# RWKV gate product in split operands with its last 32 rows stacked three times, and rate products without 64 unread columns

## The reference, cut to what matters

```python
xx = time_shift(x) - x
xr, xw, xk, xv, xa, xg = [x + xx * mu[n] for n in range(6)]
r, k, v = jnp.einsum('nbtc,ncd->nbtd', jnp.stack([xr, xk, xv]), w_rkv)
w = -jax.nn.softplus(-(w0 + jnp.tanh(xw @ w1) @ w2)) - 0.5
a = jax.nn.sigmoid(a0 + (xa @ a1) @ a2)
g = jax.nn.sigmoid(xg @ g1) @ g2          # g1: 1024 x 160, g2: 160 x 1024
...
_, y = lax.scan(step, S0, ...)            # per head, state 64 x 64
y = group_norm(y) * gn_g + gn_b + bonus
return (y * g) @ w_o
```

## Time and profile before

| | |
|---|---|
| median of 3 runs | 1249.38 us (1249.12 to 1252.03) |
| the profiled execution | 1249.55 us, span 1247.4 us |
| mean granted TensorE clock | 0.981 |
| TensorE busy | 1179.5 us, 95% of the span |
| VectorE busy | 749.7 us, 60% |
| ScalarE busy | 596.4 us, 48% |
| GpSimd busy | 107.1 us, 9% |

### The profile page before, as it was taken

One profiled execution on the slowest core, in us unless ns is written; L12 is line 12 of the kernel. 1 busy time (PEld: TensorE's weight loads), 2 busy tenths in 40 slices (PEclk: granted clock), 3 DMA queues, 4 the chain that ended last, 5 costly groups with the idle time before them and its releaser, 6 DMA issues.

```text
span 1247.4 us, 24447 instructions
## 1 busy us (share of the span) xinstructions
PE 1179.5 (95%) x10438; PEld 1054.7 (85%) x10438; DVE 749.7 (60%) x1078; ACT 596.4 (48%) x837; POOL 107.1 (9%) x87
## 2 busy tenths in 40 slices
PE   4999989989999999999999999799999998999997
PEld 4897777669999989877899999599988787999996
DVE  7888665364554466775555545767587553655554
ACT  4574543354434355554644344475555554544343
POOL 0032253501100000220010000000000000000000
PEclk9999999989999999999899999899999999999999
DMA  8431011046454545232455446335433342455550
GB/s 324 170 115 70 4 50 51 16 175 233 177 195 181 214 145 203 102 136 102 169 202 184 187 177 228 135 136 203 143 116 123 115 180 85 172 200 191 181 200 34
DMA packets 29417, 187.86 MB, mean 151 GB/s; under 512 B 3344, under 2 KB 5264, under 8 KB 8080
## 3 DMA queue, kind: packets, MB, share of 16 engines
q1 hardware_dynamic: 26544, 176.94, 38.6%
q10 hardware_dynamic: 2784, 9.60, 2.2%
HBM read 185.49 MB, written 1.05 MB: 150 GB/s over the span
## 4 chain that ended last, share of the span: by engine, by line
PE 83%; DVE 9%; ACT 5%; issue 2%; DMA 0%; POOL 0%; DVEq 0%; ACTq 0%; SPq 0%; POOLq 0%
PE ps L1914 24%; PE ps L1916 23%; PE ps L1915 23%; DVE w_lo L1248 2%; ACT w_hi L575 1%; PE ps L2032 1%; PE ps L2216 1%; ACT ma_s L986 1%; PE ps L2221 1%; PE ps L2218 1%; DVE mix_lo L1683 1%; DVE x_tm L1482 1%; PE ps L2362 1%; PE ps L2164 1%; PE ps L2612 1%
## 5 line engine op out<-in xcount | busy, mean ns | idle before, releaser
L1248 DVE TENSOR_TENSOR w_lo<-w_raw,w_hi 128x2048 fp32r<-128x2048 f32 x160 | 373.5, 2350 | 179.1 <-ACT w_hi L575 178.5
L1914 PE MATMUL ps<-x_hi,w_hi 128*128 128x256 f32 x1344 | 382.9, 285 | 4.2 <-DVE x_lo L1520 2.2
L575 ACT CAST w_hi<-w_raw 128x2048 fp32r<-128x2048 f32 x158 | 300.7, 1906 | 177.8 <-PE ps L1916 174.4
L1915 PE MATMUL ps<-x_lo,w_hi 128*128 128x256 f32 x1344 | 379.3, 282 | 0.0
L1916 PE MATMUL ps<-x_hi,w_lo 128*128 128x256 f32 x1344 | 379.2, 282 | 0.0
L1914 PEld LDWEIGHTS ps<-x_hi,w_hi 128*128 128x128 f32 x1344 | 257.2, 191 | 11.3 <-issue 9.5
L1915 PEld LDWEIGHTS ps<-x_lo,w_hi 128*128 128x128 f32 x1344 | 257.1, 191 | 2.2 <-issue 0.7
L1916 PEld LDWEIGHTS ps<-x_hi,w_lo 128*128 128x128 f32 x1344 | 257.0, 191 | 0.0
L1914 PE MATMUL ps<-w_hi,hid_hi 128*128 128x512 f32 x304 | 119.8, 394 | 0.1
L1916 PE MATMUL ps<-w_hi,hid_lo 128*128 128x512 f32 x304 | 119.4, 393 | 0.0
L1915 PE MATMUL ps<-w_lo,hid_hi 128*128 128x512 f32 x304 | 118.4, 390 | 0.0
(11 more groups left out here) (367 smaller groups left out, 1716.8 us busy)
## 6 DMA issues: line engine op xcount, KB each, us to landing
w_raw<-in_weights SPq DMA_DIRECT2D x164, 1024.0 KB, 4.8
xt<-in_xT SPq DMA_DIRECT2D x2, 512.0 KB, 5.7
x_tm<-in_x SPq DMA_DIRECT2D x1, 1024.0 KB, 4.8
gain<-in_mix_g ACTq DMA_DIRECT2D x2, 512.0 KB, 4.6
gain<-in_mix_b ACTq DMA_DIRECT2D x2, 512.0 KB, 5.6
gain<-in_ffn_g ACTq DMA_DIRECT2D x2, 512.0 KB, 7.1
gain<-in_ffn_b ACTq DMA_DIRECT2D x2, 512.0 KB, 8.8
gain<-in_mem ACTq DMA_DIRECT2D x1, 1024.0 KB, 4.8
```

Of the source, the lines that this page charges most:

```text
L575: nc.scalar.copy(w_hi[:, i % WS, :], w_raw[:, i % RAW, :]).then_inc(hi_done, 1)
L1248: V.tensor_tensor(w_lo[:, i % WS, :], w_raw[:, i % RAW, :], w_hi[:, i % WS, :].bitcast(F32), ALU.subtract).then_inc(lo_done, 1)
L1914: nc.tensor.matmul(out, hi_l, hi_r, start=start, stop=False)
L1915: nc.tensor.matmul(out, hi_l, lo_r, start=False, stop=False)
```

## The change

The gate product is computed in split operands. The 128 rows take three fp32r products with `g2_hi`, `g2_lo`, `sig_hi` and `sig_lo`. The 32 rows take one product: hi, lo and hi of the activations stand under each other in 96 rows of `sig_b`, and hi, hi and lo of the weights in 96 rows of `g2b_s`, so that one contraction over 96 rows adds all three terms. For that `load_g` brings the 32 rows three times. ScalarE (`gate_high`) rounds and VectorE (`gate_low`) subtracts, in slot 5 of the next group's loop, and after the loop for group 3; the activations are split once, in slot 5 of g = 0. The raw `g2`, `g2b`, `sig_g`, `sig_g2` and `y_last` now lie in tiles that are free by then (`sw`, `sa_m`, `av`), so the first gate load waits for `S_BK` of group 0, and each later one for the subtraction of the group before.

In `S_BA0` and `S_BA1` the moving operand leaves out its first 64 columns, which nobody reads: 192 columns in place of 256. `S_KA0` and `S_KA1` keep 256.

```diff
+LORA_B = GLORA - P
+GB = 3 * LORA_B
...
-            sig_g = sb("sig_g", [P, T], where=a_rw)
-            sig_g2 = sb("sig_g2", [GLORA - P, T], where=a_rw)
+            sig_hi = sb("sig_hi", [P, T], F32R, a_rw)
+            sig_b = sb("sig_b", [GB, T], F32R, a_rw)
...
-                for dst, src in ((g2, d["g2"][0:P]), (g2b, d["g2"][P:GLORA])):
-                    sp.dma_start(dst[:, :], src[:, at]).then_inc(gate_lora_loaded, 16)
+                sp.dma_start(g2, d["g2"][0:P, at]).then_inc(gate_lora_loaded, 16)
+                for n in range(3):
+                    sp.dma_start(g2b[LORA_B * n:LORA_B * n + LORA_B], d["g2"][P:GLORA, at]).then_inc(gate_lora_loaded, 16)
...
-                if i == 11:
-                    sp.wait_ge(lora1_mm, 2)
-                    sp.wait_ge(mix_lo_done, 4)
-                    load_g(0)
+            sp.wait_ge(side_ready, side_at(0, S_BK) + 1)
+            load_g(0)
...
-                sp.wait_ge(side_ready, side_at(g - 1, S_G) + 1)
+                sp.wait_ge(gate_lo_done, g)
                 load_g(g)
...
+                    if (g, k) == (0, C_SA0):
+                        act.wait_ge(sig_lo_done, 1)
...
+            def gate_high(g):
+                if g:
+                    act.wait_ge(side_ready, side_at(g - 1, S_G) + 1)
+                act.wait_ge(gate_lora_loaded, 64 * (g + 1))
+                nc.scalar.copy(g2_hi[:, :], g2)
+                nc.scalar.copy(g2b_s[:, :], g2b[0:GB]).then_inc(gate_hi_done, 1)
...
+                    if g and slot == 5:
+                        gate_high(g - 1)
+                    elif slot == 5:
+                        nc.scalar.copy(sig_hi[:, :], sig_g)
+                        nc.scalar.copy(sig_b[2 * LORA_B:GB, :], sig_g2)
+                        nc.scalar.copy(sig_b[0:LORA_B, :], sig_g2).then_inc(sig_hi_done, 1)
...
             side_step(3, S_BK)
+            gate_high(3)
...
+            def gate_low(g):
+                dve.wait_ge(gate_hi_done, g + 1)
+                V.tensor_tensor(g2_lo[:, :], g2, g2_hi[:, :].bitcast(F32), ALU.subtract)
+                low = g2b_s[2 * LORA_B:GB, :]
+                V.tensor_tensor(low, g2b[2 * LORA_B:GB], low.bitcast(F32), ALU.subtract).then_inc(gate_lo_done, 1)
...
+                    if g and slot == 5:
+                        gate_low(g - 1)
+                    elif slot == 5:
+                        dve.wait_ge(sig_hi_done, 1)
+                        V.tensor_tensor(sig_lo[:, :], sig_g, sig_hi[:, :].bitcast(F32), ALU.subtract)
+                        V.tensor_tensor(sig_b[LORA_B:2 * LORA_B, :], sig_g2, sig_b[0:LORA_B, :].bitcast(F32), ALU.subtract)\
+                         .then_inc(sig_lo_done, 1)
...
+            gate_low(3)
...
-                    pe.wait_ge(gate_lora_loaded, 32 * (g + 1))
+                    pe.wait_ge(sig_lo_done, 1)
+                    pe.wait_ge(gate_lo_done, g + 1)
                     for t in range(TT):
-                        mm(z[:, T * t:T * t + T], sig_g[:, tok(t)], g2[:, :], start=True, stop=False)
-                        last = mm(z[:, T * t:T * t + T], sig_g2[:, tok(t)], g2b[:, :], start=False, stop=True)
+                        three(z[:, T * t:T * t + T], sig_hi[:, tok(t)], sig_lo[:, tok(t)], g2_hi[:, :], g2_lo[:, :], True, False)
+                        last = mm(z[:, T * t:T * t + T], sig_b[:, tok(t)], g2b_s[:, :], start=False, stop=True)
...
+                    c0 = HB if k in (S_BA0, S_BA1) else 0
...
-                            last = mm(both[q][:, T * m:T * m + T], src[f, 2 * m + t, :],
-                                      ar[f, 2 * g + m, t, :, :].rearrange("p s c -> p (s c)"), start=True, stop=True)
+                            last = mm(both[q][:, T * m + c0:T * m + T], src[f, 2 * m + t, :],
+                                      ar[f, 2 * g + m, t, :, :].rearrange("p s c -> p (s c)")[:, c0:T], start=True, stop=True)
```

More of the change, by code:

```diff
@@ L229, in build @@
                 akrk_b = sb("akrk_b", [P, TT, 4, 2, P], where=a)
-                g2 = sb("g2", [P, 256], where=a)
-                g2b = sb("g2b", [GLORA - P, 256], where=a)
+                g2_hi = sb("g2_hi", [P, 256], F32R, a)
+                g2_lo = sb("g2_lo", [P, 256], F32R, a)
                 gn_g = sb("gn_g", [P, 256], where=a)
@@ L235, in build @@
                 bk_tm = sb("bk_tm", [P, 2, 2, P], where=a)
-                y_last = sb("y_last", [P, TT * 4, HD], where=a)
+                sig_lo = sb("sig_lo", [P, T], F32R, a)
+                g2b_s = sb("g2b_s", [GB, 256], F32R, a)
                 u_m = sb("u_m", [P, 256], where=a)
@@ L248, in build @@
                                 for n, m in ((0, TT), (1, TT * 4), (2, 2), (3, TT * 4)))
+            y_last = av[:, 0:4, :].rearrange("p a (b c) -> p (a b) c", c=HD)
+            g2, g2b = (sw[:, n:n + 2, :].rearrange("p a b -> p (a b)") for n in (0, 2))
+            sig_g, sig_g2 = sa_m[:, 0, :], sa_m[0:LORA_B, 1, :]
             y_last_sq = cum[:, :, :].rearrange("p a (b c) -> p (a b) c", c=HD)
@@ L337, in build @@
         mixed_ready = sem("mixed_ready")
+        gate_hi_done, gate_lo_done, sig_hi_done, sig_lo_done = (
+            sem(n) for n in ("gate_hi_done", "gate_lo_done", "sig_hi_done", "sig_lo_done"))
         mix_hi_done, mix_lo_done = sem("mix_hi_done"), sem("mix_lo_done")
@@ L762, in _ @@
             act.wait_ge(lora1_mm, 2)
-            nc.scalar.activation(sig_g[:, :], ps[:, 5, 0:T], ACT.Sigmoid)
-            nc.scalar.activation(sig_g2[:, :], ps[0:GLORA - P, 5, T:2 * T], ACT.Sigmoid).then_inc(lora1_out, 1)
+            nc.scalar.activation(sig_g, ps[:, 5, 0:T], ACT.Sigmoid)
+            nc.scalar.activation(sig_g2, ps[0:LORA_B, 5, T:2 * T], ACT.Sigmoid).then_inc(lora1_out, 1)
             take_rates(3)
```

## The result

| | before | after |
|---|---|---|
| median of 9 runs each, taken together | 1246.10 us (1242.60 to 1252.03) | 1240.55 us (1235.98 to 1247.31) |
| ratio after/before, 95% interval | | 0.995 (0.9932 to 0.9969) |
| the profiled execution | 1249.55 us, span 1247.4, clock 0.981 | 1240.55 us, span 1238.7, clock 0.984 |

The change takes 5.6 us between these medians, or by the ratio 6.2 (3.9 to 8.5), and 5.9 was forecast. 1246.1 less 5.9 is 1240.2.

A forecast was written before the change was run, and what follows sets the result against it. TensorE, 83% of the chain that ended last, was taken to bound the kernel. Savings of 4.9 (gate product) and 1.4 us (pairs) less 0.4 of costs made 5.9, from 1249.55 to 1243.6 us, range 1241.3 to 1247.2.

The forecast's parts named there:

- the base: The time subtracted from: the profiled execution's 1249.55 us, taken as close to the three runs' median of 1249.38.
- rival 2: Shorter gate product and a wait drop TensorE's clock in slots 8 and 9 of g = 3; 1.3 us lost, chance 0.15.
- The range: Whole kernel: 1241.3 us at the low end to 1247.2 at the high end.
- The gate product: Four places, three in the RWKV loop and one in the last chain: 2.50 to 1.15 us each, 4.9 us saved together.
- Group 2's product: Slot 7 of g = 3: 0.8 us saved, not 1.36, since the next product waits for VectorE's addition.
- The count of passes: A skill page's four passes for float32, one for reduced: the four gate products would save at most 3.4 us.
- The pairs: S_BA0 and S_BA1, eight times in the loop: 0.2 us a step, seven count, 1.4 us saved.
- `S_BA0` of g = 2: The one narrowed step that buys nothing, since the next pair waits 0.41 us for VectorE.
- The costs: New ScalarE copies and VectorE subtractions, in slot 5 and before the last chain: 0.4 us lost in all.
- The pair of g = 1 behind the masks: VectorE's pair behind slot 6's masks: 0.15 of 1.1 us lateness reaches it; the place costs 0.2 us.
- `sig_lo` of g = 0: VectorE's subtractions for the activations in g = 0: hidden, cost nothing; 0.8 us without that cover.
- The loads: Gate loads on SyncE's queue, issued well ahead of their first reader: cost nothing.

The follow-up runs named there:

- e2_gate: The changed kernel with all 256 columns in S_BA0 and S_BA1, so the split gate product alone; 1243.10 us, ratio 0.997.
- e5_unstacked: The changed kernel with the 96-row product replaced by three over 32 rows, high parts only; 1245.87 us, ratio 0.999.
- e1_pairs: The kernel before with one edit, 192 columns in place of 256 in S_BA0 and S_BA1; 1245.57 us, ratio 0.9986.
- e3_wires: The changed kernel with 256 columns in S_BA0 and S_BA1 and a float32 gate product of high parts only, keeping loads, copies and subtractions; 1247.34 us, ratio 1.0002.
- a1_change: The changed kernel unaltered, run again beside the kernel before; 1239.76 us over 4 runs, ratio 0.9928.
- a2_change: The changed kernel unaltered, run once more for a narrower ratio; 1242.02 us over 12 runs, ratio 0.9956.
- e10_change_kept: The changed kernel with unread products before long waits of the last chain and norms, none in slot 7, a repeat; 1239.94 us, ratio 0.9938.
- b0_before: The kernel before, unaltered, run once for a second profile; 1247.78 us.
- e9_before_warm: The kernel before with unread products before long waits of the last chain and norms, and behind S_BON in slot 7; 1242.88 us, ratio 0.9968.
- e11_before_kept: The kernel before with unread products before long waits of the last chain and norms, none in slot 7; 1244.75 us, ratio 0.9977.
- e8_change_warm: The changed kernel with unread products before long waits of the last chain and norms, and behind S_BON in slot 7; 1240.33 us, ratio 0.9944.
- e6_kept_warm: The changed kernel with unread products before long waits of the last chain and norms, none in slot 7, first run; 1237.04 us, ratio 0.9921.

## Why the prediction was wrong, and where it was right

**The step that failed: the base.** "Its time is 0.17 us over the median of the three runs, 1249.38, which makes no difference." The three runs and the profiled execution agreed with each other, and all four lay high. Of the 98 runs of the kernel before that went with the experiments, 21 are at 1249.12 us or more, and their medians are 1247.2, 1247.6, 1247.0 and 1247.1. The nine runs of the result have 1246.1, so the base was 3.45 us over the kernel that the change was measured against, while the change itself, 5.6 to 6.2 us, was as forecast. The profile showed a reason: a mean clock of 0.981, with stretches at 0.60 and 0.57. At 7 us for 0.01 that is 2.8 us above an execution at 0.985, and 2.1 above the mean clock of the 98 runs, 0.984. The rest of the 3.45 is that the nine runs came out some 1 us lower than the other groups, which no forecast could know. The forecast used those stretches only to ask whether the change would add one (rival 2), not whether the execution it subtracted from held more of them than usual.

**The range** had the costs of the change in it and 1.3 us for one vanished stretch, but not the level of the kernel itself. One program runs from 1241.1 to 1255.6 us, and medians of 9 to 29 runs of it differ by up to 1.5 us. A low end that allowed for 3 us in the base would have been about 1238. There is also a slip in it: it was added up from 1249.38 us, and from 1249.55, the base of the sum, the same terms give 1241.45.

**The gate product**, 4.9 less 0.4, was right: 4.3 us in e2_gate at one clock. The product takes 1.22 us, forecast 1.15. The 96-row matmul is at the pitch of the 128-row one, the value that was taken between bounds; e5_unstacked shows that 32-row products are not. Group 2's product gave 1.03 us in place of 0.8, but its slot 6 took 0.30 longer (2.41 to 2.71 us). From slot 6 to slot 8 of g = 3 it was 5.77 us and is 4.98, 0.79 less, where 0.8 less 0.1 of costs was forecast.

**The count of passes**, by which the four products would save at most 3.4 us, gave too little: 2.50 - 1.22 = 1.28 us a product, measured, with nearly all of it carried through. The Trainium skill, "FP8 and Floating Point Precision", section TensorE Precision Notes, counts four passes for float32; the trace has five times the pitch, 0.62 against 0.12 us.

**The pairs**, 1.4 us, were right: 1.3 in e1_pairs, and 1.07 to 0.85 us a step. That `S_BA0` of g = 2 buys nothing was right too: slots 1 and 2 of that group take 8.63 us after and also in e2_gate, which has all 256 columns.

**The costs**, 0.4 us, were about right as a sum (0.8 in e3_wires, within what the measurement can tell) but not by their terms. The pair of g = 1 behind the masks, which was to be 0.15 us late, was not late at all; and `sig_lo` of g = 0, called nothing, took 1.50 us beside GpSimd's work. Place by place: the loop of g = 0 fell from 32.05 to 31.84 us, where its two narrower pairs alone give 0.44. The other 0.23 us is slot 6 behind the split activations: 3.64 us in all eight profiles that have both parts of the change, 3.41 before. The loads were hidden, as said: no copy of a gate operand waits in the profile after, and ScalarE takes group 3's at 216.34 right behind its copy of `bk_tm`.

**The clock**, rival 2: the place that it named, slots 8 and 9 of g = 3, now at 212 to 216, is at full clock in after, a1_change, a2_change and e10_change_kept. But some 5 us behind the product, at the start of the last chain, the clock fell in two of the nine profiles that have it in split operands: 216 to 220 is at 0.67 in a1_change and at 0.81 in e10_change_kept. In a1_change the first 2.2 us of that chain became 3.6, the 1.3 us of the rival's price. In none of the six profiles with the float32 product (before, b0_before, e1_pairs, e3_wires, e9_before_warm, e11_before_kept) did it fall there. Two in nine against none in six can be chance; whether the shorter product makes this stretch likelier is not shown, and not excluded.

**What stays open.** Why one execution has a low stretch in a place and the next has none was not settled. Nor was what the pauses of TensorE at full clock are, for which the profile names no wait (0.67 us in e8_change_warm, some 0.7 in e6_kept_warm).

## What to carry to other kernels

Before subtracting a sum from one profiled execution, look at the mean granted clock and the low stretches in it. They are part of the base, and a few runs that agree with each other can all lie on one side. Where the clock wanders, compare kernels at one clock; here the whole change came out at 7.4, 5.0 and 5.6 us by medians, and at 5.2, 5.4 and about 6 at one clock. A pair of profiles without low stretches shows the terms one by one. And a short contraction beside full ones is worth stacking: as three products of its own it cost 0.75 us a token half here, and stacked into one 0.24.

## What the runs showed of the hardware

- A matmul of 256 fp32r columns has the same pitch of 0.12 us over 96 rows as over 128. Over 32 rows amid products over 128, the change to them and back costs 0.27 us on top.
- VectorE's subtraction of two operands that both lie in SBUF takes 0.42 us alone and 1.16 to 1.50 us while GpSimd works on SBUF (0.94 where the two overlap in part). An addition that reads PSUM stayed at 0.42 us beside the same GpSimd product. So a hole in VectorE's line is only worth its length if GpSimd is quiet in it.
- The time of this kernel falls by about 7 us for each 0.01 of mean granted clock, and its executions have 0.974 to 0.991 in the kernel before. With a correlation of -0.89 to -0.92 that goes with some four fifths of the variance from run to run.
- With unread products in front of TensorE's waits the mean clock was 0.992 to 0.994 in place of 0.984. The kernel before was 2.4 and 4.1 us faster with them by its medians, where 7 us for 0.01 gives 5.8 and 7.3; what took the rest was not measured.
- TensorE can pause at a granted clock of 1.00 without a wait that the profile names: 0.67 us in e8_change_warm, some 0.7 in e6_kept_warm, at places where other executions have no pause.
